# Gated embedding stage: products of rounded parts and remainders, rows in four buffers, the norm two tiles ahead

## What is computed

```python
x = x + hierarchical_moe(rms_norm(x, norm_ffn[l]), ...)
ple_gate = jax.nn.sigmoid(rms_norm(x, norm_ple[l]) @ w_ple_gate[l])
x = x + ple_gate * (p[l] @ w_ple_proj[l])
```

## Time and profile before

| what | us |
|---|---|
| median of three runs (lowest, highest) | 3732.43 (3729.77, 3738.77) |
| the profiled execution's own time | 3736.39 |
| its span in the trace | 3734.4 |
| TensorE busy, share of the span | 3103.0, 83% |
| VectorE, ScalarE, GpSimd busy | 1932.1, 1195.7, 601.4 |
| mean granted clock | 0.896 |
| first DMA of `ple` to its last VectorE step | 2142.73 to 2328.37 |

### The profile page before, as it was taken

The page is one execution under the profiler, slowest core; times in us unless marked ns, Lnnn a source line. Parts: engine busy times, 40 slices in busy tenths (PEclk is TensorE's granted clock), DMA queues, the critical chain, the costliest instruction groups (busy, mean ns, idle before and its releaser), DMA issues. The chain is left out here.

```text
span 3734.4 us, 53365 instructions
## 1 busy us (share of the span) xinstructions
PE 3103.0 (83%) x20841; PEld 2514.0 (67%) x20841; DVE 1932.1 (52%) x2512; ACT 1195.7 (32%) x1698; POOL 601.4 (16%) x299
## 2 busy tenths in 40 slices
PE   7999968888586997599999878799998946636699
PEld 6999957777353444488788634799998835524387
DVE  3365736665462323588888633200576745566421
ACT  2000014342452112377777512211111642222310
POOL 3232201111000000322222010222221401100000
PEclk9999978899697998799999989899998967766899
DMA  4455220000205322699999642435666230031321
GB/s 170 169 202 176 101 103 15 28 28 8 75 12 218 129 86 107 212 393 399 399 399 399 258 169 74 166 105 160 197 221 217 82 132 0 0 91 30 148 90 62
DMA packets 260717, 562.92 MB, mean 151 GB/s; under 512 B 31232, under 2 KB 104832, under 8 KB 259472
## 3 DMA queue, kind: packets, MB, share of 16 engines
q1 hardware_dynamic: 210304, 443.86, 33.2%
q10 hardware_dynamic: 40384, 82.65, 6.0%
q0 software_dynamic: 9872, 34.23, 2.5%
HBM read 437.66 MB, written 121.84 MB: 150 GB/s over the span
## 5 line engine op out<-in xcount | busy, mean ns | idle before, releaser
L360 PE MATMUL pin_psum<-pin_sb_w,pin_sb_hT 128*128 128x354 f32 (+1 forms) x5376 | 975.6, 343 | 25.9 <-DVE pin_sb_w L322 21.4
L360 PEld LDWEIGHTS pin_psum<-pin_sb_w,pin_sb_hT 128*128 128x128 f32 x5376 | 936.5, 189 | 61.8 <-DVE pin_sb_w L322 22.2
L3884 DVE TENSOR_TENSOR moe_sb_wlo<-moe_sb_raw,moe_sb_whi 128x2048 fp32r<-128x2048 f32 x192 | 437.7, 2287 | 92.5 <-ACT moe_sb_whi L3709 92.4
L3709 ACT ACTIVATE moe_sb_whi<-moe_sb_raw 128x2048 fp32r<-128x2048 f32 x192 | 367.2, 1916 | 133.3 <-DMA moe_sb_raw<-in_w_gate 46.7
L294 ACT ACTIVATE pin_sb_xt<-pin_psum,pin_sb_ss 128x353 f32<-128x353 f32 (+1 forms) x112 | 63.7, 588 | 563.9 <-PE pin_psum L360 491.6
L339 DVE TENSOR_SCALAR pin_sb_xt<-pin_psum,pin_sb_ss 128x353 f32<-128x353 f32 (+1 forms) x112 | 69.0, 625 | 330.6 <-PE pin_psum L360 330.3
L3952 PE MATMUL moe_psum<-moe_sb_whi,moe_sb_xhi 128*128 128x512 f32 x512 | 204.4, 399 | 15.3 <-DVE moe_sb_xlo L3888 15.3
L3952 PE MATMUL moe_psum<-moe_sb_whi,moe_sb_xlo 128*128 128x512 f32 x512 | 201.3, 393 | 0.0
L3952 PE MATMUL moe_psum<-moe_sb_wlo,moe_sb_xhi 128*128 128x512 f32 x512 | 201.2, 393 | 0.0
L253 POOL TENSOR_TENSOR pin_sb_w<-pin_sb_raw,pin_sb_w 128x2832 fp32r<-128x2832 f32 (+1 forms) x26 | 186.3, 7164 | 3.9 <-issue 0.6
L251 POOL CAST pin_sb_w<-pin_sb_raw 128x2832 fp32r<-128x2832 f32 (+1 forms) x26 | 75.8, 2916 | 642.2 <-PE pin_psum L360 595.5
(11 more groups left out here) (668 smaller groups left out, 5536.7 us busy)
## 6 DMA issues: line engine op xcount, KB each, us to landing
moe_sb_raw<-in_w_gate SPq DMA_DIRECT2D x64, 1024.0 KB, 13.9
moe_sb_raw<-in_w_up SPq DMA_DIRECT2D x64, 1024.0 KB, 14.1
moe_sb_raw<-in_w_down SPq DMA_DIRECT2D x64, 1024.0 KB, 12.6
pin_sb_raw<-in_w_in SPq DMA_DIRECT2D x16, 1412.0 KB, 8.0
scratch_proj<-pin_sb_xt ACTq DMA_DIRECT2D x16, 1412.0 KB, 6.2
pin_sb_raw<-in_w_in SPq DMA_DIRECT2D x12, 1792.0 KB, 8.9
scratch_proj<-pin_sb_xt ACTq DMA_DIRECT2D x12, 1792.0 KB, 6.3
scratch_ybuf<-moe_sb_yb ACTq DMA_DIRECT2D x32, 512.0 KB, 6.8
```

The lines of the kernel that those rows point to most:

```text
L360: mm = te.matmul(ps[:, t, 0:cols], hT[a_part][:, k, t * P:(t + 1) * P], wt[b][w_part][:, k, :], start=(k == 0 and n == 0), stop=(k == KD - ...
L3709: s.activation(whi[q][:, :, :], raw[q][:, :, :], ACT.Copy).then_inc(hi, 1)
L3884: tt(wlo[q][:, :, :], raw[q][:, :, :], whi[q][:, :, :].bitcast(F32), ALU.subtract).then_inc(lo, 1)
```

## The change

The products of `ple` are made of three instead of one, on operands of a rounded type (float32r): with a = hi + lo, the sum of a_hi*w_hi, a_hi*w_lo and a_lo*w_hi. ScalarE rounds (a Copy into the rounded type), VectorE subtracts to get the remainder, for the weights once, piece by piece, and for the turned rows in each tile. The rows of `x` and `p` have four buffers, and the sum is written over `x`. The norm is made for t+2 instead of t+1. The turn of t+1 stands between the two halves of gate product t (in tile 0 behind both). Loops are written out. SP loads the weights in ten pieces of 512 KB. GpSimd's program is unchanged. The diff, cut to its core:

```diff
+    KW, LEAD, AHEAD = KD + 2, 3, 4
-        wg = ph.sb("wg", [P, KD, D])
-        wp = ph.sb("wp", [P, 2, D])
+        raw = ph.sb("raw", [P, KW, D])
+        whi, wlo = (ph.sb(n, [P, KW, D], F32R) for n in ("whi", "wlo"))
...
@@ sync
+            def load(t):
+                b = t % AHEAD
+                if t >= AHEAD:
+                    sp.wait_ge(y_st[b], 16)
...
-            sp.dma_start(wg[:, :, :], g["w_ple_gate"].rearrange("(k p) n -> p k n", p=P)).then_inc(wg_in, 16)
-            load(1, 1)
-            sp.dma_start(wp[:, :, :], g["w_ple_proj"].rearrange("(k p) n -> p k n", p=P)).then_inc(wp_in, 16)
-            with sp.Fori(0, NT // 2 - 1) as j:
-                for b in range(2):
-                    store(2 * j + b, b)
-                    load(2 * j + b + 2, b)
...
+            for k in range(KW):
+                src = g["w_ple_gate"][k * P:(k + 1) * P, :] if k < KD else g["w_ple_proj"][(k - KD) * P:(k - KD + 1) * P, :]
+                sp.dma_start(raw[:, k, :], src).then_inc(w_in[k], 16)
+                if k == LEAD:
+                    load(1)
+            for t in range(2, AHEAD):
+                load(t)
+            for t in range(NT):
+                store(t)
+                if 1 <= t <= NT - AHEAD:
+                    load(t - 1 + AHEAD)
...
@@ scalar
+            def round_rows(t):
+                b = t % 2
+                s.wait_ge(gained.sem, gained.done(t))
+                s.activation(hThi[b][:, :, :], hT[:, :, :], ACT.Copy)
+                s.activation(pThi[b][:, :, :], blocks(ps, 2, 2), ACT.Copy).then_inc(rounded.sem, 1)
+
+            def round_weights(k):
+                s.wait_ge(w_in[k], 16)
+                s.activation(whi[:, k, :], raw[:, k, :], ACT.Copy).then_inc(w_hi, 1)
...
+            for k in range(LEAD):
+                round_weights(k)
+            norm(0)
+            for k in range(LEAD, KW):
+                round_weights(k)
+            round_rows(0)
+            norm(1)
+            for t in range(NT):
+                if t + 1 < NT:
+                    round_rows(t + 1)
+                if t + 2 < NT:
+                    norm(t + 2)
+                gate(t)
@@ vector
-                ve.tensor_copy(pT[b][:, :, :], blocks(ps, 2, 2))
-                tt(hT[:, :, :], blocks(ps, 0, 8), bcast(gcol[:, :], P), ALU.mult).then_inc(copied.sem, 1)
+                tt(hT[:, :, :], blocks(ps, 0, 8), bcast(gcol[:, :], P), ALU.mult).then_inc(gained.sem, 1)
+                ve.drain()
+                ve.wait_ge(rounded.sem, rounded.done(t))
+                tt(hTlo[b][:, :, :], hT[:, :, :], hThi[b][:, :, :].bitcast(F32), ALU.subtract)
+                tt(pTlo[b][:, :, :], blocks(ps, 2, 2), pThi[b][:, :, :].bitcast(F32), ALU.subtract).then_inc(copied.sem, 1)
+
+            def rest_of_weights(k):
+                ve.wait_ge(w_hi, k + 1)
+                tt(wlo[:, k, :], raw[:, k, :], whi[:, k, :].bitcast(F32), ALU.subtract).then_inc(w_lo, 1)
...
-                ve.wait_ge(y_st[b], 16 * n + 16)
-                tt(y[b][:, :], xt[b][:, :], m[:, :], ALU.add).then_inc(added.sem, 1)
+                tt(x_t[:, :], x_t[:, :], m[:, :], ALU.add).then_inc(added.sem, 1)
...
+            for k in range(LEAD):
+                rest_of_weights(k)
             ve.wait_ge(const_in, 32)
             ve.wait_ge(table_in, 32)
+            norm(0)
+            for k in range(LEAD, KW):
+                rest_of_weights(k)
+            copy(0)
+            norm(1)
+            for t in range(NT):
+                if t + 1 < NT:
+                    copy(t + 1)
+                if t + 2 < NT:
+                    norm(t + 2)
+                finish(t)
@@ tensor
+            def product(bank, a, b, k0, n_k, h, k):
+                hi, lo = a
+                for i, (m, w) in enumerate(((hi[b], whi), (hi[b], wlo), (lo[b], whi))):
+                    mm = te.matmul(ps[:, bank + h, :], m[:, k, :], w[:, k0 + k, h * 512:(h + 1) * 512],
+                                   start=(k == 0 and i == 0), stop=(k == n_k - 1 and i == 2))
                 return mm
...
                 te.wait_ge(copied.sem, copied.done(t))
                 te.wait_ge(gates.sem, gates.done(t - 1))
-                product(4, hT, wg, KD).then_inc(gate_sums.sem, 1)
-                if not last(t):
-                    turn(t + 1, 1 - b, n + b)
+                if first(t):
+                    for k in range(KD):
+                        te.wait_ge(w_lo, k + 1)
+                        for h in range(2):
+                            mm = product(4, gate_rows, b, 0, KD, h, k)
+                    mm.then_inc(gate_sums.sem, 1)
+                    te.wait_ge(w_lo, KW)
+                    turn(t + 1)
+                else:
+                    for k in range(KD):
+                        product(4, gate_rows, b, 0, KD, 0, k)
+                    if not last(t):
+                        turn(t + 1)
+                    for k in range(KD):
+                        mm = product(4, gate_rows, b, 0, KD, 1, k)
+                    mm.then_inc(gate_sums.sem, 1)
                 te.wait_ge(added.sem, added.done(t - 1))
-                product(6, pT[b], wp, 2).then_inc(proj_sums.sem, 1)
+                for h in range(2):
+                    for k in range(2):
+                        mm = product(6, proj_rows, b, KD, 2, h, k)
+                mm.then_inc(proj_sums.sem, 1)
```

More of the change, by code:

```diff
@@ L874, in ple @@
         gcol = ph.sb("gcol", [P, KD])
-        wg = ph.sb("wg", [P, KD, D])
-        wp = ph.sb("wp", [P, 2, D])
+        raw = ph.sb("raw", [P, KW, D])
+        whi, wlo = (ph.sb(n, [P, KW, D], F32R) for n in ("whi", "wlo"))
         two = lambda n, shape: [ph.sb(f"{n}{b}", shape) for b in range(2)]
-        xt = two("xt", [P, D])
-        pt = two("pt", [P, 2, P])
+        xt = [ph.sb(f"xt{b}", [P, D]) for b in range(AHEAD)]
+        pt = [ph.sb(f"pt{b}", [P, 2, P]) for b in range(AHEAD)]
         junk = ph.sb("junk", [P, D])
@@ L883, in ple @@
         hT = ph.sb("hT", [P, KD, P])
-        pT = two("pT", [P, 2, P])
+        hThi, hTlo = ([ph.sb(f"{n}{b}", [P, KD, P], F32R) for b in range(2)] for n in ("hThi", "hTlo"))
+        pThi, pTlo = ([ph.sb(f"{n}{b}", [P, 2, P], F32R) for b in range(2)] for n in ("pThi", "pTlo"))
         sg = ph.sb("sg", [P, D])
         m = ph.sb("m", [P, D])
-        y = two("y", [P, D])
         di = ph.sb("di", [P, 2, NT], I32)
@@ L910, in store @@
+            def store(t):
                 sp.wait_ge(added.sem, added.done(t))
-                sp.dma_start(out[bass.ds(t * P, P), :], y[b][:, :]).then_inc(y_st[b], 16)
-            for b in range(2):
-                sp.sem_inc(y_st[b], 16)
-            load(0, 0)
+                sp.dma_start(out[t * P:(t + 1) * P, :], xt[t % AHEAD][:, :]).then_inc(y_st[t % AHEAD], 16)
+            load(0)
             for dst, src in ((ident[:, :], g["ident"]), (gcol[:, :], g["norm_ple"].rearrange("(k p) -> p k", p=P))):
@@ L930, in _ @@
+            for t in range(NT):
+                store(t)
+                if 1 <= t <= NT - AHEAD:
+                    load(t - 1 + AHEAD)
+            for b in range(AHEAD):
+                sp.wait_ge(y_st[b], 16 * NT // AHEAD)
         @blk.gpsimd
@@ L957, in body @@
                 s.activation(sg[:, :], banks(ps, 4), ACT.Sigmoid).then_inc(gates.sem, 1)
-            for c in (squared, root, gates):
+            for c in (squared, root, rounded, gates):
                 c.begin(s)
-            norm(0, 0, 0)
-            each_tile(s, body)
+            for k in range(LEAD):
[11 more added lines that the diff above has]
+                gate(t)
         @blk.vector
@@ L975, in weigh, with norm @@
                         ve.drain()
-                    ins = ve.scalar_tensor_tensor(xt[b][:, :], yb[b][k][:, :], wts[:, k, one], xt[b][:, :], ALU.mult, ALU.add)
+                    ins = ve.scalar_tensor_tensor(xt[b][:, :], yb[c][k][:, :], wts[:, k, t:t + 1], xt[b][:, :], ALU.mult, ALU.add)
                 ins.then_inc(weighed.sem, 1)
-            def norm(t, b, n):
-                weigh(t, b, n)
+            def norm(t):
+                b = t % 2
+                weigh(t)
                 ve.drain()
@@ L1006, in body, with turn @@
                 ve.drain()
[L1007 to L1010 removed]
+                tt(x_t[:, :], x_t[:, :], m[:, :], ALU.add).then_inc(added.sem, 1)
+            for c in (mean, normed, gained, copied, added, weighed):
                 c.begin(ve)
+            for k in range(LEAD):
+                rest_of_weights(k)
             ve.wait_ge(const_in, 32)
             ve.wait_ge(table_in, 32)
[L1014 to L1016 removed]
+            norm(0)
[9 more added lines that the diff above has]
+                finish(t)
         @blk.tensor
         def _(te):
[L1020 removed]
+            def turn(t):
+                b = t % AHEAD
                 te.wait_ge(normed.sem, normed.done(t))
@@ L1027, in turn, with body @@
                 mm.then_inc(turned.sem, 1)
[L1029 to L1033, removed]
-                return mm
```

(20 more changed lines are left out.)

51 lines of the change are left out of this document (23 added, 28 removed).

## The result

The changed kernel takes 3749.72 us (median of nine runs, 3743.29 to 3755.22), the kernel before 3733.75 (nine runs of the same series, 3729.2 to 3742.86): ratio 1.0041, 95% interval 1.0028 to 1.0053. It is 16 us slower. The forecast was 3751.7, 19.3 us slower, range 3740 to 3760.

What follows compares the result with a forecast made beforehand. A closed chain of waits across TensorE, VectorE and ScalarE, plus half-clock starts, was the bound. Start +6.8, tile 0 +6.9, tiles 1 to 5 +11.4, tile 6 -2.2, tile 7 -3.6 gave +19.3: 3751.7 us, range 3740 to 3760.

Steps and rivals of the forecast that it cites:

- The loop: From turn through copy, norm two ahead and sigmoid to the next gate product: 13.75 us; period 19.2 at full clock.
- The clock: After each 4.5 us TensorE stand, half clock for 4.8 us, costing 2.4 us per body; period 21.6.
- The opening: Before the first gate product: rounding, remainders and tile 0's copy queue behind the last weight piece, +6.8 us.
- Tile 0: First tile: both gate halves, a cold start and the chain of waits make 27.0 us against 20.1, +6.9.
- Tiles 6 and 7: Last two tiles: no norm delays tile 6's sigmoid, -2.2 us; tile 7 has shorter products, -3.6 us.
- The products: TensorE's new matmuls 0.2267 us apart: 13.6 us per tile instead of 17.2, 14.7 with the turn.
- the stands: Sign: TensorE idle 4 to 5 us before gate products 2 to 6, some 10 before tile 1's.
- the clock (near 0.88): Sign: TensorE's granted clock near 0.88 over the tiles with stands, instead of 1.00.
- the bodies: Sign: stretches between starts of successive gate products last 21 to 22 us.
- The second rival: TensorE's stands don't bring the clock down: +7.3 us, or 3740; chance 0.15.
- The third rival: Rows of x land more than 5 us later, moving the weighing: +31 us, or 3764; chance 0.05.

Runs made afterwards that it cites:

- gate_first: Changed kernel with the sigmoid of t ahead of norm(t+2) on ScalarE; 3713.04 us, ratio 0.9931 to the kernel before; measured again, 0.9946.
- turn_first: Changed kernel with the turn of t+1 ahead of both halves of gate product t on TensorE; 3730.24 us, ratio 0.9978 to the kernel before.
- clock_filled: Changed kernel with 116 unread matmuls added on TensorE after the projections to fill its stands; 3740.36 us, ratio 1.0008 to the kernel before.
- copy_early: Changed kernel with tile 0's copy and rounding ahead of weight pieces 3 to 9; 3745.04 us, ratio 1.0021 to the kernel before.
- old_products: Changed kernel with one float32 matmul in place of three, rows' remainders left out of the product; ratio 1.0047 to the kernel before.
- norm_one_ahead: Changed kernel with the norm made for t+1 again and the turn behind both gate halves; 3730.82 us, ratio 0.9985 to the kernel before.

## Why the prediction was right

The forecast was right in direction and in mechanism, and within 3.3 us in the difference of medians (16.0 against 19.3). By the trace it was less close: the stage grew by 14.2, not 19.3. The runs of one kernel lie up to 14 us apart, so the nearer hit of the medians is partly luck. Step by step:

- **The loop.** The chain from the turn to the next gate product was put at 13.75 us; from 2230.43 to 2243.89 it is 13.46. gate_first and turn_first cut it at either end and TensorE took 15.1 and 15.8 per tile; clock_filled left it closed and the bodies were 19.1, against the 19.2 that the prediction gave for full clock. Shown. Two small errors cancel in it: the chain is 0.3 shorter than put, the first half at full clock 0.25 longer (5.7, not 5.44).
- **The clock.** The direction was right, the size not: 2.4 us per body were forecast from lows of 4.4 to 5.15 us behind longer stands and at starts. Behind the regular stands of 3.8 us the clock was half for 3.3 us, not 4.8, and the first half took 7.2 against 5.7, so 1.5 us; behind the 8.3 us stand ahead of tile 1 the clock was half for over 5.6 us, and that body lasted 21.80, 2.7 over the 19.1 at full clock. This is the term that was mis-sized most: tiles 1 to 5 cost 104.5 - 96.6 = +7.9, not +11.4.
- **The opening.** +6.8 forecast; from the first DMA to the first product 36.32 against 29.21, +7.1. The last weight piece was there at 2169.28, when its rounding starts, 29.7 after the first DMA and so about when it landed before; the other 6.6 us are the chain behind it. copy_early took 6.1 of it back, so the queueing of tile 0's copy behind the weights is shown.
- **Tile 0.** 25.46 against 20.12, +5.3, not +6.9. The chain is shorter there than I put it: no sigmoid has run yet, and the root shows no table load ahead of it (1.28 us).
- **Tiles 6 and 7.** 16.72 against 19.3, -2.6 (forecast -2.2); from the gate product of tile 7 to the end 16.82 against 20.39, -3.6 as forecast.
- **The products.** Matmuls were put at 0.2267 apart; in this stage they are 0.233: the first half of a gate product takes 5.7 us at the full clock up to its turn's start, not 5.44, and a tile with its turn 15.1, not 14.7. In tiles 1 to 5 it hardly shows, and neither does the gain itself: old_products gives it back for 2 us by the runs (6 by the profile), while in the open loop it is worth 21 to 26.

The sum by measured terms is +7.1 +5.3 +7.9 -2.6 -3.6 = +14.1, the stage's 14.2. Of the signs named in advance, the stands (4 to 5 us and some 10) came out at 3.8 and 8.3, the clock (near 0.88) at 0.92 in tiles 2 to 5, and the bodies (21 to 22 apart) at 20.7: all near, all on the side of a milder clock.

The second rival (the clock holds) gave +7.3. clock_filled makes that case and fills the stand ahead of tile 1 as well, which the rival priced at 2.3: +5.0, or 1.0013, inside the measured 0.9997 to 1.0018. The third rival, late rows, did not occur.

The Trainium skill's passage on HAM oscillation (TensorE: Matmul & The Clock Gate), that a burst which waits starts again at the half clock, fits the body of tile 1 (0.50 over its first 5.6 us). In tiles 2 to 6 it fits the cost but not the moment: these bodies start at the full clock and fall to half within about 1 us, with a mean of 0.76 over the first half. The Trainium skill's 131 ns for back-to-back 512-column matmuls (the same page, Back-to-back issue gap) is not met: the last stage has 227 ns and this one 233.

## What to carry to other kernels

When a stage's bottleneck engine is made faster, follow the loop from its output back to its next input through every engine's written order: a step placed "ahead" for a later tile delays whatever stands behind it on the same engine, here the sigmoid behind the norm two tiles on. A gain per instruction is worth its face value only while that engine never waits; measure the order first, then the instruction. Two reorderings that each open a loop can close another one together, as the sigmoid first and the turn first did here, so try them singly and jointly.

## What had not been expected of the hardware

A shorter product made a body longer: with float32 products TensorE stood 2 us per body, the granted clock stayed at 1.00 and bodies were 20.4 apart; with the faster ones it stood 3.8 us, the first half ran at a mean of 0.76 and bodies were 20.7 apart. Stands of 2.3 us lowered the clock behind two of the seven in norm_one_ahead (0.70 over the first 5.7 us) and left it at 1.00 behind the others; the one in gate_first, ahead of tile 1, lowered it as well (0.70). What decides it no run here shows. Filling the stands with 116 matmuls that nobody reads gave 12 us. A stand of 3.8 us cost 1.5 us in the body behind it, less than the 2.2 to 2.7 that the earlier trace rows had suggested, and the clock fell only after TensorE was at work again.
